# Weight loads of an expert stage with neighbouring rows on one partition, gate and up kept apart

## The chip, the core and the metric

The kernel runs on one core of a Trainium2 chip. The metric is the device time of one execution in microseconds; what is compared is the median of several runs. Engines are PE (TensorE), ACT (ScalarE), DVE (VectorE), POOL (GpSimd) and SP (SyncE, which here only issues transfers). All arithmetic is in float32, the large products in three passes over operands split in a high and a low part.

## What is computed

The reference is one layer of a streaming encoder on 1024 + 64 tokens of width 1024: a layer norm, a token mixing (state space and short convolution), a second layer norm, and a mixture of 64 experts of width 256. Only the experts bear on the change:

```
scores = sigmoid(h @ w_router); top_e, w = 6 of 64 experts for each token, gates normalised * 2.5
for each expert e, over the tokens that chose it:
    hid = silu(x @ w_gate[e]) * (x @ w_up[e])        # 1024 -> 256, twice
    y   = (hid @ w_down[e]) * gate                   # 256 -> 1024
f[token] = sum of its y + shared expert
```

Gate and up weights of an expert are (1024, 256) each, its down weights (256, 1024): 1 MB each, 3 MB for one expert, 192 MB in all.

## The kernel before

The stages follow each other: trunk, mixing, output (which also computes the routing scores, the shared expert and the slot lists), routing, expert, final. The change touches the routing stage and the expert stage.

**Blocks.** Tokens are gathered by expert in blocks of up to 128. An expert has as many blocks as its tokens need, at least one; here 76 blocks, and the loop runs over 77 (an even count of trips after the first). Most experts have one block, some two. Every engine runs the same loop over blocks (`over_blocks`), three of them written out (`HEAD = 3`), the rest in a hardware loop with two blocks a trip.

**Transfers of weights.** SP loads them on its own queue. `raw_up` has three slots (`UP_SLOTS`), each with gate and up of one expert side by side, `raw_dn` two (`DN_SLOTS`). The routing stage issues the loads of experts 0 to 2 (L1514, down of 0 and 1 at L1519), the expert stage the rest (`gate_up` with L1656, `down` with L1664), in the order down of e-3, gate of e, up of e. Before it issues a load, SP waits until the slot is free (`up_l_done`, `dn_l_done`, counted in blocks by a table) and until the load of the same kind for the expert before has landed. A weight matrix is viewed as `(k p) n -> p k n`: row 128k + p goes to partition p. So a partition gets eight rows of 256 values for gate and for up, each row a run of 1 KB, and two rows of 1024 values for down, each a run of 4 KB. In `raw_up` the row k of gate stands next to row k of up, 512 values.

**One block.** ACT copies the weights to `up_h` in two calls of 2048 values a partition (`up_high`, L1687; half 0 has rows k = 0 to 3 of both gate and up, half 1 the others), DVE subtracts to get `up_l` (`up_low`, L1858), both two blocks ahead of the product. `up_high_first` waits for gate and for up before half 0. Down weights are handled alike (`down_high` L1728, `down_low` L1878), in the block itself. PE's order in a block n (`body`) is: `up(n)`, 24 matmuls of 128 x 512 (L1801); `turn_x(n+1)`, 8 transposes of the gathered tokens (L1820), where the token tile `xg` is the operand loaded as weights and the identity is the moving one; `down(n-1)`, 12 matmuls (L1813); `turn_hid(n)`, 2 transposes of the hidden values (L1828). ACT takes the silu of the gate half (L1703) and copies transposes out (L1714, L1720) and results out (L1708); DVE makes `hid` (L1850) and the low parts (L1866, L1872).

**Tokens.** POOL gathers the rows of a block from `tok` by an indirect transfer (L1759) and scatters the results with an addition to `acc` (L1770). These use a queue of their own on the same DMA engines. In POOL's order of a block stand the scatter of block n-1 and then the gather of block n+3; a scatter is issued only when the scatter before has landed, since both may add to the same rows. PE's `turn_x` waits for the gather.

Of the kernel before, what the change touches and what calls it, by code (L numbers as in the profile page):

```python
# [6 lines left out]
ALU = mybir.AluOpType  # L7
ACT = mybir.ActivationFunctionType
F32 = mybir.dt.float32
F32R = mybir.dt.float32r  # L10
# [3 lines left out]
P = 128  # L14
D = 1024
KD = D // P
# [19 lines left out]
D_EXP = 256  # L36
ROUTED_SCALE = 2.5
IN_RING = 3
UP_SLOTS = 3
# [1450 lines left out]
def routing_stage(nc, io, keep, rt):  # L1490

    with ExitStack() as ctx:
        m = Pools(nc, ctx, "route")
# [14 lines left out]
        @block.sync  # L1508
        def _(sp):
            for e in range(UP_SLOTS):  # L1510
                for side, src, sem in ((0, io.w_gate, rt.gate_in), (1, io.w_up, rt.up_in)):
                    if e:
                        sp.wait_ge(sem, 16 * e)
                    sp.dma_start(rt.raw_up[:, e, :, D_EXP * side:D_EXP * (side + 1)],  # L1514
                                 src[0, e].rearrange("(k p) n -> p k n", p=P)).then_inc(sem, 16)
                if e < DN_SLOTS:
                    if e:
                        sp.wait_ge(rt.down_in, 16 * e)
                    sp.dma_start(rt.raw_dn[:, e, :, :], io.w_down[0, e].rearrange("(k p) n -> p k n", p=P)).then_inc(  # L1519
                        rt.down_in, 16)  # L1520

        @block.gpsimd
# [65 lines left out]
def expert_stage(nc, io, keep, rt):  # L1588

    with ExitStack() as ctx:  # L1590
        m = Pools(nc, ctx, "moe")
        raw_up, raw_dn = rt.raw_up, rt.raw_dn
        up_h, up_l = m.sb("up_h", [P, 2, KD, 2 * D_EXP], F32R), m.sb("up_l", [P, 2, KD, 2 * D_EXP], F32R)
        idx_g, idx_s = m.sb("idx_g", [P, 2], I32), m.sb("idx_s", [P, 2], I32)
        xg = m.sb("xg", [P, 2, D])
        x_h, x_l = m.sb("x_h", [P, 2, KD, P], F32R), m.sb("x_l", [P, 2, KD, P], F32R)
        sg = m.sb("sg", [P, 2, D_EXP])
        hid = m.sb("hid", [P, 2, D_EXP])
# [3 lines left out]
        p_gu = m.ps("p_gu", [P, 2, 512])  # L1602
        p_dn = m.ps("p_dn", [P, 2, 512])
        p_tr = m.ps("p_tr", [P, 2, 512])
        p_ht = m.ps("p_ht", [P, 512])
# [7 lines left out]
        gate_in, up_in, down_in = rt.gate_in, rt.up_in, rt.down_in  # L1613
        go, act_go, sp_go, zeroed = (m.sem(n) for n in ("go", "act_go", "sp_go", "zeroed"))
        block = ctx.enter_context(nc.Block())
        w_g = io.w_gate[0].rearrange("e (k p) n -> e p k n", p=P)
        w_u = io.w_up[0].rearrange("e (k p) n -> e p k n", p=P)
        w_d = io.w_down[0].rearrange("e (k p) n -> e p k n", p=P)
        HEAD = 3
        HALF = KD // 2  # L1620

        def wait(eng, sem, value):

# [24 lines left out]
        @block.sync  # L1648
        def _(sp):
            def gate_up(e, slot, until):  # L1650
                wait(sp, up_l_done, until)
                sp.sem_inc(sp_go, 1)
                for half, src, sem in ((0, w_g, gate_in), (1, w_u, up_in)):
                    wait(sp, sem, e * 16)
                    sp.sem_inc(sp_go, 1)
                    sp.dma_start(raw_up[:, slot, :, D_EXP * half:D_EXP * (half + 1)],  # L1656
                                 src[at(e)].rearrange("a p k n -> (a p) k n")).then_inc(sem, 16)

            def down(e, slot, until):
                wait(sp, dn_l_done, until)  # L1660
                sp.sem_inc(sp_go, 1)
                wait(sp, down_in, e * 16)
                sp.sem_inc(sp_go, 1)
                sp.dma_start(raw_dn[:, slot, :, :], w_d[at(e)].rearrange("a p k n -> (a p) k n")).then_inc(down_in, 16)  # L1664

            def ends(e):
                return entry(sp, 3, e, P)

            AHEAD = UP_SLOTS + DN_SLOTS
            LOOP = UP_SLOTS * DN_SLOTS  # L1670
            peeled = N_EXP - (N_EXP - AHEAD) // LOOP * LOOP
            for e in range(UP_SLOTS, peeled):
                if e >= AHEAD:
                    down(e - UP_SLOTS, (e - UP_SLOTS) % DN_SLOTS, ends(e - AHEAD))
                gate_up(e, e % UP_SLOTS, ends(e - UP_SLOTS))
            with sp.Fori(peeled, N_EXP - LOOP + 1, LOOP) as b:
                for u in range(LOOP):
                    down(b + (u - UP_SLOTS), (peeled + u - UP_SLOTS) % DN_SLOTS, ends(b + (u - AHEAD)))
                    gate_up(b + u, (peeled + u) % UP_SLOTS, ends(b + (u - UP_SLOTS)))
            for e in range(N_EXP - UP_SLOTS, N_EXP):  # L1680
                down(e, e % DN_SLOTS, ends(e - DN_SLOTS))

        @block.scalar
        def _(act):
            def up_high(n, par, slot, half):
                ks = slice(HALF * half, HALF * (half + 1))
                act.activation(up_h[:, par, ks, :],  # L1687
                               raw_up[:, bass.ds(slot, 1), ks, :].rearrange("p a k n -> p (a k) n"),
                               ACT.Copy).then_inc(up_h_done, 1)

            def up_high_first(n, par):
# [100 lines left out]
        @block.tensor  # L1792
        def _(pe):
            def up(n, par):
                wait(pe, xl_done, n + 1)
                wait(pe, up_l_done, n + 1)
                wait(pe, hid_done, n - 1)
                terms = [(x[:, par, k, :], w[:, par, k, :]) for k in range(KD)
                         for x, w in ((x_h, up_h), (x_h, up_l), (x_l, up_h))]
                for i, (x, w) in enumerate(terms):  # L1800
                    mm = pe.matmul(p_gu[:, par, :], x, w, start=(i == 0), stop=(i == len(terms) - 1))  # L1801
                mm.then_inc(up_done, 1)

            def down(n, par):
                wait(pe, dn_l_done, n + 1)
                wait(pe, hidl_done, n + 1)
                wait(pe, y_act, n)
                for h in range(2):
                    cols = slice(512 * h, 512 * (h + 1))
                    terms = [(a[:, par, k, :], w[:, par, k, cols]) for k in range(2)  # L1810
                             for a, w in ((hid_h, dn_h), (hid_h, dn_l), (hid_l, dn_h))]
                    for i, (a, w) in enumerate(terms):
                        mm = pe.matmul(p_dn[:, h, :], a, w, start=(i == 0), stop=(i == len(terms) - 1))  # L1813
                mm.then_inc(down_done, 1)

            def turn_x(n, par):
                wait(pe, gathered[par], dma_count(n, par))
                wait(pe, xl_done, n)
                for k in range(KD):
                    tr = pe.transpose(p_tr[:, k // 4, (k % 4) * P:(k % 4 + 1) * P], xg[:, par, k * P:(k + 1) * P],  # L1820
                                      keep.ident[:, :])
                tr.then_inc(x_turned, 1)

            def turn_hid(n, par):
                wait(pe, hid_done, n + 1)
                wait(pe, hidl_done, n)
                for k in range(2):
                    tr = pe.transpose(p_ht[:, k * P:(k + 1) * P], hid[:, par, k * P:(k + 1) * P], keep.ident[:, :])  # L1828
                tr.then_inc(hid_turned, 1)

            def body(n, par):
                first = isinstance(n, int) and n == 0
                if first:
                    turn_x(0, 0)
                up(n, par)
                turn_x(n + 1, 1 - par)
                if not first:
                    down(n - 1, 1 - par)
                turn_hid(n, par)
            last = over_blocks(pe, body)  # L1840
            down(last + 0, 0)

        @block.vector
        def _(v):
            tt, stt = v.tensor_tensor, v.scalar_tensor_tensor
# [7 lines left out]
            def up_low(n, par, halves=(0, 1)):  # L1853
                slot = entry(v, 1, n, UP_SLOTS - 1)
                for half in halves:
                    ks = slice(HALF * half, HALF * (half + 1))
                    wait(v, up_h_done, n * 2 + (half + 1))
                    low = tt(up_l[:, par, ks, :], raw_up[:, bass.ds(slot, 1), ks, :].rearrange("p a k n -> p (a k) n"),  # L1858
                             up_h[:, par, ks, :].bitcast(F32), ALU.subtract)
                if 1 in halves:  # L1860
                    low.then_inc(up_l_done, 1)

# [107 lines left out]
def build(nc, args):  # L1970

    io = Names()
# [24 lines left out]
    with ExitStack() as ctx:  # L1997
        m = Pools(nc, ctx, "keep")
        keep = Names()
# [32 lines left out]
        with ExitStack() as moe:  # L2032
            r = Pools(nc, moe, "rt")
            rt = Names()
            rt.idx = r.sb("idx", [P, P], I32)
            rt.wgt = r.sb("wgt", [P, P])
            rt.tab = r.sb("tab", [1, 5, P + 8], I32)
            rt.raw_up = r.sb("raw_up", [P, UP_SLOTS, KD, 2 * D_EXP])
            rt.raw_dn = r.sb("raw_dn", [P, DN_SLOTS, 2, D])
            rt.gate_in, rt.up_in, rt.down_in = r.sem("gate_in"), r.sem("up_in"), r.sem("down_in")  # L2040
            routing_stage(nc, io, keep, rt)
            expert_stage(nc, io, keep, rt)
# [32 lines left out]
```

## Time and profile before

| | us |
|---|---|
| median of 3 runs | 1703.79 |
| lowest and highest of them | 1691.95, 1705.31 |
| the profiled execution | 1694.93 |
| its span in the trace | 1693.2 |
| PE busy, with weight loads apart | 1348.9 and 1040.7 |
| DVE, ACT, POOL busy | 1108.3, 829.4, 756.3 |
| moved by DMA | 320.96 MB, mean 190 GB/s |

Busy times are sums over the whole span, and stages with different limits are mixed in them. The busy time of PE counts matmuls whose ends are modelled, so neighbours overlap; the number of matmuls in a window says more of its pace. A DMA share above 1 means that packets overlap on the engines.

### The profile page before, as it was taken

Reading aid. Unit: us, or ns where it says so; the run is one execution under the profiler, and the core shown is the slowest. Engines: PE = TensorE matmul, PEld = TensorE weight load, DVE = VectorE, ACT = ScalarE, POOL = GpSimd, SP = SyncE. Lnnn points to the kernel's source line nnn. Section 1 sums busy time; section 2 is a strip of 40 time slices with the busy share of each in tenths; the row PEclk is TensorE's granted clock in tenths of the full one; section 3 lists DMA queues with packets and bytes.
Section 4 is the critical chain, followed back from the end, with each engine's and each line's share of the span. In section 5 each row is a group of like instructions: output and inputs, shape, how many; then the busy total and the mean of one; then the engine's idle time right before and its main releaser. Section 6 shows DMA issues by size and latency. Waiting matters only on the chain. (4 is left out here: it accounts for less than half of the span.)

```text
span 1693.2 us, 22502 instructions
## 1 busy us (share of the span) xinstructions
PE 1348.9 (80%) x6080; PEld 1040.7 (61%) x6080; DVE 1108.3 (65%) x1480; ACT 829.4 (49%) x911; POOL 756.3 (45%) x811
## 2 busy tenths in 40 slices
PE   1397988987869999509899899998989888888930
PEld 1264656655558888407677677776767676667720
DVE  6931435541546777427878788878778867678858
ACT  2311101101633333017777777777767766767842
POOL 2486532501422333423445555555555545445534
PEclk9998999989879999759999999999999999999965
DMA  8223447244521211167988699979989999998743
GB/s 228 87 53 77 35 68 78 33 57 52 168 76 63 75 55 59 50 224 224 317 272 270 208 334 318 334 243 315 309 252 330 302 312 323 327 315 270 208 130 130
DMA packets 233486, 320.96 MB, mean 190 GB/s; under 512 B 30512, under 2 KB 192304, under 8 KB 233440
## 3 DMA queue, kind: packets, MB, share of 16 engines
q1 hardware_dynamic: 199136, 254.35, 49.9%
q0 software_dynamic: 27488, 63.16, 14.3%
q10 hardware_dynamic: 6816, 2.88, 0.8%
q8 instruction: 22, 0.36, 0.1%
q14 instruction: 24, 0.20, 0.1%
HBM read 282.87 MB, written 64.19 MB: 205 GB/s over the span
## 5 line engine op out<-in xcount | busy, mean ns | idle before, releaser
L1858 DVE TENSOR_TENSOR moe_up_l<-rt_raw_up,moe_up_h 128x2048 fp32r<-128x2048 f32 x158 | 361.4, 2289 | 108.8 <-ACT moe_up_h L1687 108.3
L1687 ACT ACTIVATE moe_up_h<-rt_raw_up 128x2048 fp32r x158 | 301.6, 1910 | 114.4 <-issue 74.8
L1801 PE MATMUL moe_p_gu<-moe_up_h,moe_x_h 128*128 128x512 f32 x616 | 251.9, 409 | 16.2 <-DVE moe_x_l L1866 16.2
L1770 POOL DMA_INDIRECT acc<-moe_y,moe_idx_s x77 | 191.5, 2487 | 134.7 <-DMA acc<-moe_y,moe_idx_s 101.9
L1801 PE MATMUL moe_p_gu<-moe_up_h,moe_x_l 128*128 128x512 f32 x616 | 244.2, 396 | 0.0
L1801 PE MATMUL moe_p_gu<-moe_up_l,moe_x_h 128*128 128x512 f32 x616 | 244.1, 396 | 0.0
L680 PE MATMUL mix_proj<-co_hT,co_win 128*128 128x384 f32 (+1 forms) x768 | 238.7, 473 | 6.5 <-PEq L102 6.5
L1878 DVE TENSOR_TENSOR moe_dn_l<-rt_raw_dn,moe_dn_h 128x2048 fp32r<-128x2048 f32 x77 | 176.8, 2296 | 66.6 <-ACT moe_dn_h L1728 64.2
L680 PEld LDWEIGHTS mix_proj<-co_hT,co_win 128*128 128x128 f32 x768 | 146.7, 192 | 94.9 <-issue 9.6
L1765 POOL COPY moe_idx_s<-rt_idx 128x1 int32 (+1 forms) x77 | 79.5, 1032 | 221.9 <-ACT moe_y L1708 221.9
L1728 ACT ACTIVATE moe_dn_h<-rt_raw_dn 128x2048 fp32r x77 | 148.0, 1922 | 25.1 <-DMA rt_raw_dn<-in_w_down_dram 19.2
L1813 PE MATMUL moe_p_dn<-moe_dn_h,moe_hid_h 128*128 128x512 f32 x308 | 135.4, 440 | 25.1 <-DVE moe_dn_l L1878 25.0
L1801 PEld LDWEIGHTS moe_p_gu<-moe_up_h,moe_x_h 128*128 128x128 f32 x616 | 116.3, 189 | 48.6 <-DVE moe_x_l L1866 23.7
L1820 PE MATMUL moe_p_tr<-keep_ident,moe_xg 128*128 128x128 f32 x624 | 86.4, 283 | 69.9 <-DMA moe_xg<-tok,moe_idx_g 69.7
L1759 POOL DMA_INDIRECT moe_xg<-tok,moe_idx_g x80 | 111.3, 1391 | 65.9 <-POOL moe_idx_g L1756 62.0
L1714 ACT ACTIVATE moe_x_h<-moe_p_tr 128x512 fp32r<-128x512 f32 x156 | 84.7, 596 | 101.8 <-PE moe_p_tr L1820 97.4
L1801 PEld LDWEIGHTS moe_p_gu<-moe_up_h,moe_x_l 128*128 128x128 f32 x616 | 116.1, 189 | 28.2
L1801 PEld LDWEIGHTS moe_p_gu<-moe_up_l,moe_x_h 128*128 128x128 f32 x616 | 116.6, 189 | 24.7
L1820 PEld LDWEIGHTS moe_p_tr<-keep_ident,moe_xg 128*128 128x128 f32 x624 | 72.2, 144 | 92.6 <-DMA moe_xg<-tok,moe_idx_g 87.5
L1813 PE MATMUL moe_p_dn<-moe_dn_l,moe_hid_h 128*128 128x512 f32 x308 | 127.7, 415 | 0.0
L1813 PE MATMUL moe_p_dn<-moe_dn_h,moe_hid_l 128*128 128x512 f32 x308 | 127.6, 414 | 0.0
L1866 DVE TENSOR_TENSOR moe_x_l<-moe_p_tr,moe_x_h 128x512 fp32r<-128x512 f32 x156 | 100.2, 684 | 21.1 <-ACT moe_x_h L1714 19.0
(399 smaller groups left out, 2332.2 us busy)
## 6 DMA issues: line engine op xcount, KB each, us to landing
rt_raw_up<-in_w_gate_dram SPq DMA_DIRECT2D x64, 1024.0 KB
rt_raw_up<-in_w_up_dram SPq DMA_DIRECT2D x64, 1024.0 KB
rt_raw_dn<-in_w_down_dram SPq DMA_DIRECT2D x64, 1024.0 KB
co_win<-in_w_in_dram SPq DMA_DIRECT2D x16, 512.0 KB
resid<-trunk_x SPq DMA_DIRECT2D x9, 512.0 KB, 2.6
proj_res<-resid SPq DMA_DIRECT2D x9, 512.0 KB
tok<-proj_x POOLq DMA_DIRECT2D x9, 512.0 KB
acc<-proj_x POOLq DMA_DIRECT2D x9, 512.0 KB
```

Source lines behind the costliest of these rows:

```text
L680: mm = pe.matmul(proj[:, pn % 3, 0:ln], win[:, i % RING, k, :], hT[:, k, lo:lo + ln], start=(k == 0), stop=(k == KD - 1))
L1687: act.activation(up_h[:, par, ks, :], raw_up[:, bass.ds(slot, 1), ks, :].rearrange("p a k n -> p (a k) n"), ACT.Copy).then_inc(up_h_done, 1)
L1714: act.activation(x_h[:, par, 4 * h:4 * h + 4, :], p_tr[:, h, :].rearrange("p (k t) -> p k t", k=4), ACT.Copy).then_inc(xh_done, 1)
L1728: act.activation(dn_h[:, par, :, :], raw_dn[:, bass.ds(slot, 1), :, :].rearrange("p a k n -> p (a k) n"), ACT.Copy).then_inc(dn_h_done, 1)
L1759: pool.indirect_dma_start(out=xg[:, par, :], out_offset=None, in_=io.tok, in_offset=bass.IndirectOffsetOnAxis(ap=idx_g[:, par:par + 1], ax ...
L1770: pool.indirect_dma_start(out=io.acc, in_=y[:, par, :], in_offset=None, out_offset=bass.IndirectOffsetOnAxis(ap=idx_s[:, par:par + 1], axi ...
L1801: mm = pe.matmul(p_gu[:, par, :], x, w, start=(i == 0), stop=(i == len(terms) - 1))
L1813: mm = pe.matmul(p_dn[:, h, :], a, w, start=(i == 0), stop=(i == len(terms) - 1))
L1820: tr = pe.transpose(p_tr[:, k // 4, (k % 4) * P:(k % 4 + 1) * P], xg[:, par, k * P:(k + 1) * P], keep.ident[:, :])
L1858: low = tt(up_l[:, par, ks, :], raw_up[:, bass.ds(slot, 1), ks, :].rearrange("p a k n -> p (a k) n"), up_h[:, par, ks, :].bitcast(F32), AL ...
L1866: low = tt(x_l[:, par, 4 * h:4 * h + 4, :], p_tr[:, h, :].rearrange("p (k t) -> p k t", k=4), x_h[:, par, 4 * h:4 * h + 4, :].bitcast(F32) ...
L1878: tt(dn_l[:, par, :, :], raw_dn[:, bass.ds(slot, 1), :, :].rearrange("p a k n -> p (a k) n"), dn_h[:, par, :, :].bitcast(F32), ALU.subtrac ...
```

## The change

The views of the weights become `(p k) n -> p k n`: partition p gets the rows 8p to 8p + 7 of gate and of up, one run of 8 KB each, and the rows 2p and 2p + 1 of down, also 8 KB. In `raw_up`, `up_h` and `up_l` gate and up stand apart, each with its eight rows in one piece; the two calls of a copy or a subtraction take gate and up in place of the lower and the upper rows. A matmul of the up product reads row k of both, two runs of 256 values. As the inner index of the products is now 8p + k (2p + k for down), the transposes take each eighth column of `xg` from k on and each second of `hid`.

```diff
@@ routing stage
-                    sp.dma_start(rt.raw_up[:, e, :, D_EXP * side:D_EXP * (side + 1)],
-                                 src[0, e].rearrange("(k p) n -> p k n", p=P)).then_inc(sem, 16)
+                    sp.dma_start(rt.raw_up[:, e, side, :, :],
+                                 src[0, e].rearrange("(p k) n -> p k n", p=P)).then_inc(sem, 16)
...
-                    sp.dma_start(rt.raw_dn[:, e, :, :], io.w_down[0, e].rearrange("(k p) n -> p k n", p=P)).then_inc(
+                    sp.dma_start(rt.raw_dn[:, e, :, :], io.w_down[0, e].rearrange("(p k) n -> p k n", p=P)).then_inc(
@@ expert stage
-        up_h, up_l = m.sb("up_h", [P, 2, KD, 2 * D_EXP], F32R), m.sb("up_l", [P, 2, KD, 2 * D_EXP], F32R)
+        up_h, up_l = m.sb("up_h", [P, 2, 2, KD, D_EXP], F32R), m.sb("up_l", [P, 2, 2, KD, D_EXP], F32R)
...
-        w_g = io.w_gate[0].rearrange("e (k p) n -> e p k n", p=P)
-        w_u = io.w_up[0].rearrange("e (k p) n -> e p k n", p=P)
-        w_d = io.w_down[0].rearrange("e (k p) n -> e p k n", p=P)
+        w_g = io.w_gate[0].rearrange("e (p k) n -> e p k n", p=P)
+        w_u = io.w_up[0].rearrange("e (p k) n -> e p k n", p=P)
+        w_d = io.w_down[0].rearrange("e (p k) n -> e p k n", p=P)
...
-                    sp.dma_start(raw_up[:, slot, :, D_EXP * half:D_EXP * (half + 1)],
+                    sp.dma_start(raw_up[:, slot, half, :, :],
...
-                ks = slice(HALF * half, HALF * (half + 1))
-                act.activation(up_h[:, par, ks, :],
-                               raw_up[:, bass.ds(slot, 1), ks, :].rearrange("p a k n -> p (a k) n"),
+                act.activation(up_h[:, par, half, :, :],
+                               raw_up[:, bass.ds(slot, 1), half, :, :].rearrange("p a k n -> p (a k) n"),
...
-                terms = [(x[:, par, k, :], w[:, par, k, :]) for k in range(KD)
+                terms = [(x[:, par, k, :], w[:, par, :, k, :]) for k in range(KD)
...
-                    mm = pe.matmul(p_gu[:, par, :], x, w, start=(i == 0), stop=(i == len(terms) - 1))
+                    mm = pe.matmul(p_gu[:, par, :].rearrange("p (a n) -> p a n", a=2), x, w, start=(i == 0), stop=(i == len(terms) - 1))
...
-                    tr = pe.transpose(p_tr[:, k // 4, (k % 4) * P:(k % 4 + 1) * P], xg[:, par, k * P:(k + 1) * P],
+                    tr = pe.transpose(p_tr[:, k // 4, (k % 4) * P:(k % 4 + 1) * P], xg[:, par, k:D:KD],
...
-                    tr = pe.transpose(p_ht[:, k * P:(k + 1) * P], hid[:, par, k * P:(k + 1) * P], keep.ident[:, :])
+                    tr = pe.transpose(p_ht[:, k * P:(k + 1) * P], hid[:, par, k:D_EXP:2], keep.ident[:, :])
...
-                    ks = slice(HALF * half, HALF * (half + 1))
...
-                    low = tt(up_l[:, par, ks, :], raw_up[:, bass.ds(slot, 1), ks, :].rearrange("p a k n -> p (a k) n"),
-                             up_h[:, par, ks, :].bitcast(F32), ALU.subtract)
+                    low = tt(up_l[:, par, half, :, :],
+                             raw_up[:, bass.ds(slot, 1), half, :, :].rearrange("p a k n -> p (a k) n"),
+                             up_h[:, par, half, :, :].bitcast(F32), ALU.subtract)
...
-            rt.raw_up = r.sb("raw_up", [P, UP_SLOTS, KD, 2 * D_EXP])
+            rt.raw_up = r.sb("raw_up", [P, UP_SLOTS, 2, KD, D_EXP])
```

## Rows read from the trace of the kernel before

**Rows 1.** The page: DMA share in 40 slices of the span, and packets.
```profile
DMA  8223447244521211167988699979989999998743
...
DMA packets 233486, 320.96 MB, mean 190 GB/s; under 512 B 30512, under 2 KB 192304, under 8 KB 233440
```
**Rows 2.** Instructions of line L1703, the silu, one for each block.
```profile
L1703 ACT ACTIVATE moe_sg<-moe_p_gu x77: 357/383/392, 770.7 to 1613.1; 128x256 f32<-128x256 f32 x77
```
**Rows 3.** Windows: us; PE, PEld, DVE, ACT, POOL busy (count); PE clock, DMA share, GB/s.
```profile
1573.52:1613.13 39.61, 38.89 (x186) 30.97 (x185) 35.10 (x29) 32.94 (x33) 22.15 (x17) 1.00 0.56 155
...
1338.08:1508.40 170.32, 148.47 (x648) 117.17 (x647) 122.41 (x100) 115.02 (x113) 84.88 (x58) 0.93 1.01 318
...
770.66:1613.13 842.47, 755.51 (x3486) 600.25 (x3485) 662.01 (x531) 624.01 (x608) 429.46 (x300) 0.98 0.92 288
```
**Rows 4.** Timeline of SP: first and last gate load of the saturated stretch.
```profile
1338.08 0.37 SPq L1656 DMA_DIRECT2D rt_raw_up<-in_w_gate_dram  x1
...
1508.40 0.37 SPq L1656 DMA_DIRECT2D rt_raw_up<-in_w_gate_dram  x1
```
**Rows 5.** Waits from 780 to 1640 us: total us, times, longest.
```profile
POOL acc L1770 <- DMA acc<-moe_y,moe_idx_s: 101.9, 42, 4.7
...
PE moe_p_tr L1820 <- DMA moe_xg<-tok,moe_idx_g: 53.6, 38, 3.1
...
ACT moe_up_h L1687 <- DMA rt_raw_up<-in_w_up_dram: 23.9, 21, 4.0
...
ACT moe_dn_h L1728 <- DMA rt_raw_dn<-in_w_down_dram: 19.2, 17, 3.2
ACT moe_up_h L1687 <- DMA rt_raw_up<-in_w_gate_dram: 15.7, 17, 4.0
```
**Rows 6.** Waits of SP's queue, whole span.
```profile
SPq L1652 <- DVE moe_up_l L1858: 197.6, 34, 19.9
```
**Rows 7.** DMA from 741.6 to 744.4 us, then from 747.8 to 748.9 us.
```profile
DMA packets 966, 0.98 MB, mean 351 GB/s; under 512 B 13, under 2 KB 964, under 8 KB 966
...
q1 hardware_dynamic: 966, 0.98, 109.1%
...
DMA packets 111, 0.44 MB, mean 401 GB/s; under 512 B 1, under 2 KB 4, under 8 KB 111
...
q1 hardware_dynamic: 111, 0.44, 100.6%
```
**Rows 8.** Timeline of SP: loads of the routing stage, start us and us.
```profile
739.53 0.37 SPq L1514 DMA_DIRECT2D rt_raw_up<-in_w_up_dram  x1
742.48 0.37 SPq L1519 DMA_DIRECT2D rt_raw_dn<-in_w_down_dram  x1
745.49 0.37 SPq L1514 DMA_DIRECT2D rt_raw_up<-in_w_gate_dram  x1
748.49 0.37 SPq L1514 DMA_DIRECT2D rt_raw_up<-in_w_up_dram  x1
```
**Rows 9.** Groups by line, whole span: busy us, mean ns; idle before.
```profile
L1858 DVE TENSOR_TENSOR moe_up_l<-rt_raw_up,moe_up_h 128x2048 fp32r<-128x2048 f32 x158 | 361.4, 2289 | 108.8 <-ACT moe_up_h L1687 108.3
...
L1801 PE MATMUL moe_p_gu<-moe_up_h,moe_x_h 128*128 128x512 f32 x616 | 251.9, 409 | 16.2 <-DVE moe_x_l L1866 16.2
...
L1801 PE MATMUL moe_p_gu<-moe_up_h,moe_x_l 128*128 128x512 f32 x616 | 244.2, 396 | 0.0
...
L1820 PEld LDWEIGHTS moe_p_tr<-keep_ident,moe_xg 128*128 128x128 f32 x624 | 72.2, 144 | 92.6 <-DMA moe_xg<-tok,moe_idx_g 87.5
...
L269 PEld LDWEIGHTS trunk_pst<-keep_ident,trunk_x 128*128 128x128 f32 x72 | 14.1, 223 | 33.8 <-POOL trunk_x L239 33.8
```
**Rows 10.** Timeline of POOL, two scatters, and of PE's weight loads, one block's transposes.
```profile
998.28 1.85 POOL L1770 DMA_INDIRECT acc<-moe_y,moe_idx_s  x1 [2.67 <-DMA acc<-moe_y,moe_idx_s]
...
1008.95 2.08 POOL L1770 DMA_INDIRECT acc<-moe_y,moe_idx_s  x1 [2.35 <-DMA acc<-moe_y,moe_idx_s]
...
1010.42 0.86 PEld L1820 LDWEIGHTS moe_p_tr<-keep_ident,moe_xg 128*128 128x128 f32 x8 [1.76 <-DMA moe_xg<-tok,moe_idx_g]
```

More of the change, by code:

```diff
@@ L1615, in expert_stage @@
         block = ctx.enter_context(nc.Block())
-        w_g = io.w_gate[0].rearrange("e (k p) n -> e p k n", p=P)
-        w_u = io.w_up[0].rearrange("e (k p) n -> e p k n", p=P)
-        w_d = io.w_down[0].rearrange("e (k p) n -> e p k n", p=P)
+        w_g = io.w_gate[0].rearrange("e (p k) n -> e p k n", p=P)
+        w_u = io.w_up[0].rearrange("e (p k) n -> e p k n", p=P)
+        w_d = io.w_down[0].rearrange("e (p k) n -> e p k n", p=P)
         HEAD = 3
-        HALF = KD // 2
         def wait(eng, sem, value):
```

## The prediction

> **What bounds the kernel now.** I read the page first for where the DMA engines are busy, then the expert stage in windows, then who waits for whom, then single instructions. The page shows the DMA engines nearly full from the middle of the span to shortly before its end, and 192,304 of 233,486 packets under 2 KB [rows 1]. This is the expert stage: 77 blocks, whose silu steps start from 770.7 to 1613.1 us, so 76 periods in 842.5 us, 11.08 us each [rows 2]. Three windows of it tell three things [rows 3]. From 1573.52 to 1613.13, when the weights are all but loaded (DMA share 0.56), PE holds 186 matmuls; a block has 24 + 12 + 8 + 2 = 46, so this is four blocks in 39.61 us, 9.90 us each, and PE is busy 38.89 us of it: PE in its own order is the floor. From 1338.08 to 1508.40 the DMA share is 1.01 at 318 GB/s and PE has 648 matmuls, 14 blocks in 170.32 us. There each expert has one block, and the first and last gate load of the stretch, 14 experts apart, stand at just these times [rows 4]: 12.17 us for each expert, set by the transfers. What is left, 842.5 - 170.3 = 672.2 us for 62 blocks, runs at 10.84 us, between the two. The waits name what fills it [rows 5]: ACT waits 23.9 + 15.7 + 19.2 us for weights to land, PE 53.6 us for the gathered tokens, and POOL 101.9 us for the scatter before, so the token transfers are late as well when the same engines carry weights. SP on the other hand waits 197.6 us for a free up slot [rows 6]: with experts of two blocks the loads are far enough ahead, and faster ones bring nothing there.
>
> **The transfers.** Edits of the loads (L1514, L1519, L1656, L1664 and the three views) turn 1 KB runs of gate and up into 8 KB, and 4 KB runs of down into 8 KB; bytes, issues and waits stay. Today's price is in two quiet windows [rows 7]. One holds only 1 KB packets: 351 GB/s, so with 16 engines one per 16 x 1.024/351 = 46.7 ns. The other holds nearly only 4 KB packets: 401 GB/s; 111 packets take 100.6% of 16 engines for 1.1 us, 159.5 ns each. An expert costs 2 x 1.049/0.351 = 5.98 us for gate and up and 256 x 159.5/16 = 2.55 us for down, 8.53 us. The trace shows no 8 KB load, so its cost is bounded. From above: 8 KB at the 4 KB rate, 3 x 2.55 = 7.66 us, 0.9 less. From below: the share of the 1 KB window (109.1% of 2.8 us for 966 packets) makes 50.6 ns a packet; the line through this and 159.5 ns has 36.3 ns per KB and gives 305 ns for 8 KB, 384 x 305/16 = 7.32 us, against 2048 x 50.6/16 + 2.55 = 9.03 us, 1.7 less. The line through 46.7 and 159.5 ns gives 310 ns, 7.44 us, 1.09 less. I take **1.1 us for each expert**, since 46.7 ns is the spacing that really passed.
>
> A rule speaks against this. The Trainium skill, DMA: Bandwidth & Descriptors, section Bandwidth, says that for loads from HBM the HBM side binds at about 358 GB/s for a core. By it 351 GB/s would leave 2% and nearly nothing would come of the change. The 4 KB window's 401 GB/s disagrees on this lone core, so I keep this case only as a rival.
>
> What becomes of it: in the saturated stretch every microsecond of transfer is one of time, as 12.17 - 1.1 = 11.07 us still lies over the floor of 9.90: 14 x 1.1 = **15.4 us**. In the other 62 blocks, some 45 experts (64, less 14 and those loaded before 770 us) lose 1.1 us each, 49.5 us of transfer, and the blocks stand 62 x (10.84 - 9.90) = 58 us over the floor. This can't all come back: between experts of two blocks SP waits for slots, and the token transfers keep their latency. Bounds are 0 and 49.5 us; I take a bit under half, **22 us**, as the waits for weights and those for tokens are of like size and only the first shrink by themselves. In the routing stage the first loads follow each other at 2.95 to 3.01 us [rows 8], and the stage ends only when SP has issued the last one at 748.49, since SP is behind all other engines there. Four of the loads before that have 1 KB runs: 4 x (3.0 - 2.6) = **1.5 us**.
>
> **The split of gate and up** (layouts of raw_up, up_h, up_l; L1682 to L1690, L1852 to L1859). Each ACT copy and each DVE subtraction (2289 ns [rows 9]) keeps 2048 contiguous elements. The first copy now needs gate alone, but up_high_first still waits for both, so nothing starts earlier; no wait is added either: 0. The 24 matmuls of L1801 read two runs of 256 in place of one of 512. The trace has no such read. It can't be faster than one run, and the nearest rows for what an operand may cost are the two kinds of this very matmul, 396 and 409 ns [rows 9]: 13 ns x 24 x 77 = 24 us as the upper end, as all of it would be on PE's path. I take 0, because each run is still 1 KB long.
>
> **The transposes.** The contraction is permuted, so L1820 now loads columns of xg 32 bytes apart (8 per block) and L1828 columns of hid 8 bytes apart (2 per block). They are on PE's path, between the up and the down product. Eight loads take 0.86 us together, 108 ns each [rows 10]. No strided load stands in the trace, and a stride can't make one faster. Bounds: 0, and by the slowest rows of the same load of 128 columns, 223 ns in the trunk against 144 here [rows 9], about 1.5 times, 0.5 us a block; as that row is no stride either, the rivals go to twice (+0.86 us a block) and beyond. I take 0: the load has 108 ns for 128 elements, 0.84 ns each, while the moving side takes in 512 elements in at most 396 ns, 0.77 ns each, so the weight side reads with time to spare.
>
> The Trainium skill, Advanced Engine Details and Errata, section Memory Cachelines, has a rule the other way: SBUF lines have 16 bytes, and an access to a new line each time is penalised unless two hits fall in a line. By it the 8-byte steps of hid are free and the 32-byte steps of xg pay. No run here shows it yet; by it the sum would be the first rival.
>
> **Sum.** 15.4 + 22 + 1.5 = 38.9 us. The profiled execution took 1694.93 us (span 1693.2), which gives 1656. It lies 0.5% under the median of the runs, 1703.79; scaled by 1656/1694.93 = 0.977 this is **1665 us**.
>
> **Rivals.** (1) The stride doubles the eight loads: floor 9.90 + 0.86 = 10.76 us. The stretch keeps its gain, but the 62 blocks can't go under 10.76 and have some 0.3 us of leftover waits: 62 x (11.06 - 10.84) = +14, so 14 - 15.4 - 1.5 = -3 us, scaled 1700. For: PE is the floor. Against: element rate above. (2) The slower side: the strided loads cost over twice, at three times +1.7 us a block, floor 11.6, 76 x 11.7 = 889 against 842.5, +47 - 1.5, scaled 1750; with +1.3 it is 1719. It decides from about +1.1 us a block, where the floor of 11.0 meets today's 11.08. (3) Packets of 8 KB delay the token transfers on the same engines: a scatter waits for the landing of the one before. Its starts at 998.28 and 1008.95 are 10.67 us apart with 2.35 us of that wait, and then PE waits 1.76 us for the gather before its transposes [rows 10]. If each scatter and gather pair lost 0.6 us (a packet of 8 KB before it where one of 1 or 4 KB was), the blocks outside the stretch would go from 10.84 to 11.25 us and the stretch keep half its gain: 25 - 8 - 1.5 = +16, scaled 1720. Against: engines free up 1.1 us sooner per expert. (4) 8 KB packets move no faster than 1 KB ones in a mix limited to 318 GB/s by the memory: only the 1.5 us of the routing stage, 1702.
>
> **How the numbers follow.** Forecast 0.60, (1) 0.13, (2) 0.08, (3) 0.09, (4) 0.10. The forecast's own range: without the 22 and at 0.9 us an expert 1694.93 - 14.1, scaled 1690; with all of 49.5 and 1.7 us an expert 1628; I cut it to 1642 as the floor makes the last part unlikely. The whole range takes in (1), (4) and part of (2) and (3): 1642 to 1716. A measurement here tells about 1% from no change. Faster by more: nearly all of the forecast and a little of (1), (4): 0.64. Within 1%: 0.19. Slower: (2), most of (3): 0.17.
>
> **What would show it.** Right: nearly no packets under 2 KB in the expert stage, q1 with 64 x (2048 - 256 + 256 - 128) = 122,880 packets fewer; the stretch at about 11.1 us an expert; waits of ACT for weights well below 58.8 us; eight weight loads of L1820 still in 0.86 us; first gate loads of the routing stage closer together. Wrong: loads of L1820 at twice their time with PE busy through each block (1, 2); PE's wait for the gather and POOL's for the scatter grown (3); packets of 8 KB above 360 ns each (4).

## The result and the profile after

The changed kernel takes 1757.1 us (median of 4 runs, 1753.4 to 1761.55), the kernel before 1700.65 us (median of 4 runs beside them): a ratio of 1.034, with a 95% interval of 1.029 to 1.039. The forecast was 1665 us. The profiled execution took 1753.4 us with a span of 1751.6. The kernel became slower, although its loads, where they run alone, became just as fast as forecast. Both belong together.

The page of the changed kernel: DMA share in 40 slices, packets, the two large queues (packets, MB, share of 16 engines), and groups of section 5.

```profile
DMA  7213437425512111369785887878778889977633
...
DMA packets 110606, 320.96 MB, mean 183 GB/s; under 512 B 30512, under 2 KB 61232, under 8 KB 85984
...
q1 hardware_dynamic: 76256, 254.35, 44.0%
q0 software_dynamic: 27488, 63.16, 14.5%
...
L1799 PE MATMUL moe_p_gu<-moe_up_h,moe_x_h 128*128 128x512 f32 x616 | 250.9, 407 | 10.7 <-DVE moe_x_l L1864 10.7
...
L1799 PE MATMUL moe_p_gu<-moe_up_h,moe_x_l 128*128 128x512 f32 x616 | 243.5, 395 | 0.0
```

There are 233,486 - 110,606 = 122,880 packets fewer [rows 1], the number forecast. But the DMA share is lower in most slices of the expert stage: the engines that were the bound in a part of it now stand idle in part. The matmuls take as long as before [rows 9].

The silu of the changed kernel, one for each block (min/median/max ns, first and last start), against [rows 2].

```profile
L1701 ACT ACTIVATE moe_sg<-moe_p_gu x77: 352/384/387, 765.4 to 1671.2; 128x256 f32<-128x256 f32 x77
```

Windows of the changed kernel, with the columns of [rows 3]: the whole stage, the 14 experts of the forecast's saturated stretch, three blocks near the end.

```profile
765.36:1671.17 905.81, 778.92 (x3486) 627.24 (x3485) 663.69 (x532) 627.39 (x607) 445.10 (x300) 0.95 0.80 268
1372.28:1546.72 174.44, 142.94 (x635) 113.99 (x633) 122.94 (x99) 115.58 (x112) 74.29 (x55) 0.95 0.89 310
1639.65:1671.17 31.52, 29.50 (x138) 23.62 (x137) 26.84 (x23) 24.68 (x25) 19.37 (x13) 1.00 0.48 119
```

The stage grew from 842.5 to 905.8 us, 63.3 us, which is more than all of the span's 58.4. In the stretch an expert takes 174.44/14 = 12.46 us where it took 12.17, and the engines no longer fill it (0.89 for 1.01). Something else sets the pace there, and the waits name it. Waits of the changed kernel from 780 to 1700 us (total us, times, longest), as in [rows 5].

```profile
PE moe_p_tr L1818 <- DMA moe_xg<-tok,moe_idx_g: 117.2, 53, 5.2
...
POOL acc L1768 <- DMA acc<-moe_y,moe_idx_s: 72.3, 30, 4.8
...
ACT moe_up_h L1685 <- DMA rt_raw_up<-in_w_up_dram: 0.9, 2, 0.5
ACT moe_up_h L1685 <- DMA rt_raw_up<-in_w_gate_dram: 0.5, 1, 0.5
ACT moe_dn_h L1726 <- DMA rt_raw_dn<-in_w_down_dram: 0.3, 1, 0.3
```

ACT's waits for weights fell from 58.8 to 1.7 us. PE's wait for gathered tokens grew from 53.6 to 117.2 us. With the windows this makes a balance of the stage. PE was idle for 842.5 - 755.5 = 87.0 us, of which 53.6 for tokens and 33.4 for all else; it is idle for 905.8 - 778.9 = 126.9 us now, 117.2 for tokens and 9.7 for all else. So the rest gave 23.7 us back and the tokens took 63.6. The third part is in PE's busy time, 23.4 us more for as many matmuls. 63.6 - 23.7 + 23.4 = 63.3 us.

One stall of the changed kernel, one of its longest: POOL's, SP's and PE's instructions from its timeline.

```profile
1405.49 3.51 POOL L1768 DMA_INDIRECT acc<-moe_y,moe_idx_s  x1 [0.93 <-POOL moe_idx_s L1763]
...
1407.89 0.33 SPq L1663 DMA_DIRECT2D rt_raw_dn<-in_w_down_dram  x1
...
1410.09 0.33 SPq L1655 DMA_DIRECT2D rt_raw_up<-in_w_gate_dram  x1
...
1410.57 1.06 POOL L1757 DMA_INDIRECT moe_xg<-tok,moe_idx_g  x1 [0.80 <-POOL moe_idx_g L1754]
...
1410.79 0.33 SPq L1655 DMA_DIRECT2D rt_raw_up<-in_w_up_dram  x1
...
1420.36 1.90 POOL L1768 DMA_INDIRECT acc<-moe_y,moe_idx_s  x1 [4.83 <-DMA acc<-moe_y,moe_idx_s]
...
1423.34 1.57 PEld L1818 LDWEIGHTS moe_p_tr<-keep_ident,moe_xg 128*128 128x128 f32 x8 [5.59 <-DMA moe_xg<-tok,moe_idx_g]
```

Three weight loads, down, gate and up, are issued within 3 us of the gather. PE's transposes of that gather's tokens start 1423.34 - 1410.57 = 12.8 us after its issue, 5.59 of them waited. In the block of [rows 10], before the change, it is 1010.42 - 1001.68 = 8.7 us, the latter being this row of that kernel's timeline:

```profile
1001.68 1.05 POOL L1759 DMA_INDIRECT moe_xg<-tok,moe_idx_g  x1 [0.79 <-POOL moe_idx_g L1756]
```

This pair is not the mean: over the stage the median from a gather's issue to its landing is 10.4 us in the changed kernel and, by the landings in the trace, 8.1 us before. The scatter here too waits for the landing of the one before, 14.87 us after it where it was 10.67 [rows 10], and the next gather is issued only behind it. In sum, however, POOL's wait for the scatter before fell, from 101.9 to 72.3 us; it is the gather that became later. The eight loads after the stall take 1.57 us, which leads to the clock. Two windows of the changed kernel, with the stall and behind it (the number before the DMA share is the granted clock):

```profile
1404.00:1424.00 20.00, 13.34 (x62) 10.46 (x61) 14.54 (x12) 11.55 (x11) 9.88 (x8) 0.98 0.93 338
1424.00:1434.00 10.00, 10.00 (x44) 8.30 (x43) 5.23 (x5) 7.67 (x7) 2.87 (x4) 0.86 0.82 287
```

Behind this stall part of the time runs at 1.2 GHz in place of 2.4. The clock records show the same at 16 of the 17 places in the stage where PE waited over 3 us. The time at the lower level is 96 us of the stage where it was 41 us before, and the mean granted clock 0.95 where it was 0.98. At half speed the 55 us more cost up to 27 us, an estimate of enough size for the 23.4 us that PE is busy longer.

### The profile page after: what moved, and what is told of

Same layout as the page of the kernel before. It is cut to its first block and busy times, and to the rows that moved or that the text cites. A ratio compares the mean times of both kernels' runs of the same rounds, so it can differ in the third digit from the quotient of the medians.

```text
span 1751.6 us, 22502 instructions
## 1 busy us (share of the span) xinstructions
PE 1369.3 (78%) x6080; PEld 1065.9 (61%) x6080; DVE 1110.4 (63%) x1480; ACT 832.5 (48%) x911; POOL 771.6 (44%) x811
## 2 busy tenths in 40 slices
DMA packets 110606, 320.96 MB, mean 183 GB/s; under 512 B 30512, under 2 KB 61232, under 8 KB 85984
## 5 line engine op out<-in xcount | busy, mean ns | idle before, releaser
L1768 POOL DMA_INDIRECT acc<-moe_y,moe_idx_s x77 | 210.6, 2735 | 116.1 <-DMA acc<-moe_y,moe_idx_s 72.3
L1818 PE MATMUL moe_p_tr<-keep_ident,moe_xg 128*128 128x128 f32 x624 | 101.6, 314 | 129.6 <-DMA moe_xg<-tok,moe_idx_g 129.6
L1763 POOL COPY moe_idx_s<-rt_idx 128x1 int32 (+1 forms) x77 | 71.5, 929 | 288.7 <-ACT moe_y L1706 288.7
L1818 PEld LDWEIGHTS moe_p_tr<-keep_ident,moe_xg 128*128 128x128 f32 x624 | 86.8, 198 | 155.2 <-DMA moe_xg<-tok,moe_idx_g 153.1
L1811 PE MATMUL moe_p_dn<-moe_dn_h,moe_hid_h 128*128 128x512 f32 x308 | 141.8, 460 | 6.9 <-DVE moe_dn_l L1876 6.9
L1799 PEld LDWEIGHTS moe_p_gu<-moe_up_h,moe_x_l 128*128 128x128 f32 x616 | 115.7, 188 | 28.5
L1811 PE MATMUL moe_p_dn<-moe_dn_l,moe_hid_h 128*128 128x512 f32 x308 | 132.1, 429 | 0.0
L1811 PE MATMUL moe_p_dn<-moe_dn_h,moe_hid_l 128*128 128x512 f32 x308 | 131.6, 427 | 0.0
```

Source lines behind the costliest of these rows:

```text
L1768: pool.indirect_dma_start(out=io.acc, in_=y[:, par, :], in_offset=None, out_offset=bass.IndirectOffsetOnAxis(ap=idx_s[:, par:par + 1], axi ...
L1799: mm = pe.matmul(p_gu[:, par, :].rearrange("p (a n) -> p a n", a=2), x, w, start=(i == 0), stop=(i == len(terms) - 1))
```

## The experiments

My theory (Q in the expectations): packets of 8 KB on the weight queue take time on the same 16 engines from the token queue, and POOL's order (gather behind a waiting scatter) turns that delay into idle time of PE. The rival theories: the strided transposes cost the time (S); the order in which the rows are read from memory does; or it is the loads' earlier issue, at whatever packet length. PE's wait for the gather stands in the table at the end of this section.

**The stride alone, and 8 KB without it.** In the first the before kernel gets the strided transposes; in the second the changed kernel loses them. In both the products take rows in another order than the weights lie, so the numbers computed differ, not the amount of work.

```diff
@@ stride_only, on the kernel before; no_stride is the reverse edit on the kernel after
-                    tr = pe.transpose(..., xg[:, par, k * P:(k + 1) * P], ...)
+                    tr = pe.transpose(..., xg[:, par, k:D:KD], ...)
-                    tr = pe.transpose(..., hid[:, par, k * P:(k + 1) * P], ...)
+                    tr = pe.transpose(..., hid[:, par, k:D_EXP:2], ...)
```

> Kernel before with its loads as they were, but the transposes read each eighth column of xg and each second of hid (so the products take rows in the wrong order). Theory Q (packets of 8 KB hold up the token transfers, the stride is small): eight loads at 0.97 us instead of 0.86 and two at 0.43 instead of 0.37, 0.17 us a block, at most 13 us: ratio to before 1.000 to 1.008. Theory S (the strided loads are what costs): ratio 1.02 to 1.034.

> Changed kernel with contiguous transposes (products take rows in the wrong order). Theory Q: ratio to before 1.025 to 1.034, PE's wait for the gather stays above 100 us. Theory S: ratio at most 1.005 and the wait goes.

Measured: stride alone 1699.37 us, where the kernel before took 1695.43 us beside it, ratio 1.002 (1.000 to 1.004). Groups of stride_only (busy us, mean ns), against 144 ns in [rows 9]:

```profile
L1820 PEld LDWEIGHTS moe_p_tr<-keep_ident,moe_xg 128*128 128x128 f32 x624 | 79.8, 192 | 83.1 <-DMA moe_xg<-tok,moe_idx_g 79.5
...
L1828 PEld LDWEIGHTS moe_p_ht<-keep_ident,moe_hid 128*128 128x128 f32 x154 | 30.2, 197 | 6.7 <-DVE moe_hid L1850 0.3 <-issue 0.2
```

The mean record is a third longer, 192 ns for 144, but the records overlap: eight in a row take 0.97 us where they took 0.86.

8 KB without the stride: 1752.70 us, ratio 1.036 (1.031 to 1.040), as slow as the whole change and just above the 1.034 that theory Q allowed. Its wait, from 780 to 1640 us:

```profile
PE moe_p_tr L1818 <- DMA moe_xg<-tok,moe_idx_g: 119.3, 49, 6.1
```

The loads are dearer by the stride, but the stride is not the cause: rivals (1) and (2) fall.

**The packet length.** Everything of the change stays but the length of a run. A gap in `raw_up` and `raw_dn` breaks it into pieces, of 4 KB (gap 64 bytes), or of 2 KB for gate and up and 4 KB for down (gap 32 bytes). runs_1k keeps the layout of before for gate and up (1 KB) with the new views and transposes, and 8 KB for down.

```diff
@@ runs_4k; runs_2k has [P, UP_SLOTS, 2, 4, D_HALF + 8], [P, DN_SLOTS, 2, D + 8] and q=4 for gate and up
-            rt.raw_up = r.sb("raw_up", [P, UP_SLOTS, 2, KD, D_EXP])
+            rt.raw_up = r.sb("raw_up", [P, UP_SLOTS, 2, 2, D + 16])
-            rt.raw_dn = r.sb("raw_dn", [P, DN_SLOTS, 2, D])
+            rt.raw_dn = r.sb("raw_dn", [P, DN_SLOTS, 2, D + 16])
...
-        w_g = io.w_gate[0].rearrange("e (p k) n -> e p k n", p=P)
+        w_g = io.w_gate[0].rearrange("e (p q k) n -> e p q (k n)", p=P, q=2)
...
-                    sp.dma_start(raw_up[:, slot, half, :, :],
+                    sp.dma_start(raw_up[:, slot, half, :, 0:D],
```

> Changed kernel, but each 8 KB of a partition stands in two pieces of 4 KB with a gap of 64 bytes, so that packets have 4 KB; all else as in the changed kernel. Theory Q: the token queue gets its share back, PE's wait for the gather falls to 50 to 80 us, ratio to before 0.98 to 1.01. Theory S, or that the order of rows in memory costs: ratio stays at 1.034.

> Kernel before with neighbouring rows on one partition but gate and up side by side, so that packets of gate and up have 1 KB again (down 8 KB); strided transposes. Theory Q: about as stride_only, 1.000 to 1.012. Theory S: 1.02 to 1.034. If the order of rows in memory costs, it shows here as more than stride_only.

> Changed kernel with gate and up in four pieces of 2 KB a partition and down in two of 4 KB, gaps of 32 bytes between. Theory Q (how much the token queue gets depends on the length of the weight packets): gathers move at a rate between that of 4 KB packets (16.6 packets of 4 KB in half a microsecond) and that of 1 KB (20.6), PE's wait for the gather 55 to 80 us, ratio to before 0.998 to 1.006. Rival (only 8 KB packets are special): gathers as with 4 KB, ratio 1.006.

Measured: 4 KB 1706.36 us, ratio 1.006 (1.0035 to 1.009); 1 KB 1702.95 us, 1.006 (1.003 to 1.008); 2 KB 1677.96 us, 0.986 (0.981 to 0.990), the three with PE waits of 80.4, 58.6 and 55.5 us for the gather. From 2 KB on the wait grows with the length, and the time with the wait. The wait alone does not give the time: runs_1k and runs_4k are equally slow at 58.6 and 80.4 us. 2 KB lies below the range of both theories (0.998 to 1.006, and 1.006), so its gain was forecast by neither; it is faster than the kernel before. It has most of the cheaper transfer, as the window below shows, and leaves the gather's wait where it was; ACT's waits for weights are 38.0 us for 58.8. DMA of runs_2k from 736 to 738 us, weights of 2 KB packets alone:

```profile
DMA packets 407, 0.82 MB, mean 409 GB/s; under 512 B 8, under 2 KB 8, under 8 KB 407
```

runs_1k differs from the kernel before by the order of rows in memory, the stride and the 8 KB packets of down. Together these cost 0.6%: it waits more for the gather (58.6 us for 53.6) and for the scatter (138.5 for 101.9) and a little less for weights (53.8 for 58.8). So the order of rows, which every one of these kernels has, is not the cause of the 3.4% either.

How the engines divide themselves is to be seen in windows of 1.5 us in which a gather runs beside weight loads (q1: weights, q0: tokens; packets, MB, share of 16 engines). The kernel before, 942.5 to 944:

```profile
DMA packets 325, 0.58 MB, mean 387 GB/s; under 512 B 28, under 2 KB 235, under 8 KB 325
...
q1 hardware_dynamic: 254, 0.35, 65.5%
q0 software_dynamic: 71, 0.23, 39.2%
```

runs_2k, 975.25 to 976.75, and then runs_4k, 996.25 to 997.75:

```profile
q1 hardware_dynamic: 194, 0.40, 67.9%
q0 software_dynamic: 123, 0.22, 37.7%
```

```profile
q1 hardware_dynamic: 102, 0.41, 67.7%
q0 software_dynamic: 52, 0.20, 32.3%
```

The changed kernel, 920.75 to 922.25:

```profile
DMA packets 107, 0.63 MB, mean 418 GB/s; under 512 B 10, under 2 KB 10, under 8 KB 51
...
q1 hardware_dynamic: 59, 0.46, 72.2%
q0 software_dynamic: 48, 0.17, 27.4%
```

In sum more bytes pass, 418 GB/s for 387, but the tokens' share of the engines falls from 39.2 to 27.4%. The packet records of the whole stage say the same. Token records of 4 KB are of two kinds, with medians of 159 ns for the gathers and some 328 ns for the scatters with their addition. In slices of half a microsecond with weight packets, no scatter record and at least eight gather records, the gather records are 20.4 a slice in the kernel before, 19.3 with 2 KB, 16.7 with 4 KB and 13.5 with 8 KB. (Slices with five or more give lower numbers in the same order: 18.8, 17.9, 15.7, 12.3.) A single gather record still takes 159 ns in all four kernels, which speaks against a memory that answers more slowly: fewer of them get their turn. The median from a gather's issue to its landing is 8.1, 8.0, 8.6 and 10.4 us in this order.

The Trainium skill, DMA: Bandwidth & Descriptors, section Queues, rings and completion order, says that each engine goes round the queues that have work, a whole packet of one before the next. The direction of the four windows agrees. How long a turn is remains open: a packet there holds several descriptors, and the records do not show where one ends. Turns of single records it is not, as the tokens' share of the bytes beside 1, 2, 4 and 8 KB would then be 4/5, 2/3, 1/2 and 1/3, and the windows have 0.40, 0.35, 0.33 and 0.27.

**POOL's order.** If the delay hurts because the gather stands behind a waiting scatter, putting it ahead should bring the lost gain to light.

```diff
-                if not first:
-                    scatter(n - 1, 1 - par)
                 gather(n + 3, 1 - par)
+                if not first:
+                    scatter(n - 1, 1 - par)
```

> Changed kernel, but POOL issues the gather of block n+3 before the scatter of block n-1 instead of behind it. Theory Q (with 8 KB packets the gather lands too late, being issued behind a scatter that waits for the one before): PE's wait for the gather falls from 117 us to under 20, ratio to before 0.96 to 0.985. Rival (something else of the 8 KB loads holds the blocks up, as the scatter chain alone): the wait goes elsewhere and the ratio stays above 1.02.

> Kernel before with the same swap. Theory Q: its 54 us of waits for the gather go, but the loads of 1 KB packets (ACT's 59 us of waits for weights) bind: ratio 0.97 to 0.99, above the one of the changed kernel with the swap. Rival: ratio 0.995 to 1.005, the order of the two does nothing here.

> The kernel with 4 KB packets and the swap. Theory Q: its 80 us of waits for the gather go, ratio 0.96 to 0.98, as good as the changed kernel with the swap or 0.5% better, since scatters are served sooner. Rival: as with 8 KB packets without the swap, above 1.0.

> The same with the gather ahead of the scatter. Theory Q: between 4 KB and 1 KB packets with the swap (0.969 and 0.989), nearer to the first, 0.970 to 0.978. Rival (shorter packets are better whenever the loads keep up): below 0.969.

Measured: with 8 KB 1654.84 us, 0.975 (0.971 to 0.980); the kernel before with this edit alone 1675.37 us, 0.989 (0.986 to 0.992); with 4 KB 1643.55 us, 0.969 (0.966 to 0.973); with 2 KB 1643.57 us, 0.968 (0.963 to 0.973). The last lies below the 0.970 to 0.978 of theory Q and in the range of its rival, that shorter packets are better whenever the loads keep up; its interval takes in both, and 2 and 4 KB can't be told apart here. Waits of the 8 KB one, from 780 to 1640 us:

```profile
POOL acc L1768 <- DMA acc<-moe_y,moe_idx_s: 242.5, 60, 7.2
...
ACT moe_y L1706 <- DMA acc<-moe_y,moe_idx_s: 44.0, 31, 2.9
...
PE moe_p_tr L1818 <- DMA moe_xg<-tok,moe_idx_g: 11.5, 13, 1.9
```

PE's wait for the gather went from 117.2 to 11.5 us, and the time by 102 us, from 1757.1 to 1654.84. The delay did not vanish: it moved to the scatter, for which POOL waits 242.5 us and now even ACT, before it writes results into the buffer that the scatter still reads. Most of this is beside PE's work: over the stage PE is idle for 804.8 - 748.8 = 56.0 us, where it was 126.9. The same waits of the kernel before with this edit:

```profile
ACT moe_up_h L1687 <- DMA rt_raw_up<-in_w_up_dram: 49.9, 24, 4.7
ACT moe_dn_h L1728 <- DMA rt_raw_dn<-in_w_down_dram: 35.3, 21, 4.2
...
ACT moe_up_h L1687 <- DMA rt_raw_up<-in_w_gate_dram: 14.8, 16, 4.5
```

Its gather makes PE wait no more, and the weights are the next in line, 100 us of waits. Here longer runs help: 1654.84 against 1675.37 us on the same chip, 1.2% less, with 8 KB. So the change's sign hangs on the order of two lines in POOL's program.

| packets of gate and up (down: 4 KB, in the last row 8 KB) | order of before: ratio | PE waits for gather, us | gather first: ratio |
|---|---|---|---|
| 1 KB (kernel before) | 1 | 53.6 | 0.989 |
| 2 KB | 0.986 | 55.5 | 0.968 |
| 4 KB | 1.006 | 80.4 | 0.969 |
| 8 KB (the change) | 1.034 | 117.2 | 0.975 |

2 or 4 KB with the gather first are the fastest kernels of the study, about 3% under the kernel before. Windows of the 2 KB one over its expert stage:

```profile
767.96:1560.80 792.84, 746.69 (x3488) 608.84 (x3487) 658.35 (x531) 622.03 (x608) 442.52 (x302) 0.99 0.92 306
```

792.8 us for 76 periods are 10.43 us a block, PE is busy for 746.7 of them, and the clock stays at 0.99.

## Why the prediction was wrong

**The price of a transfer: right.** The forecast had 310 ns for a packet of 8 KB and 1.09 us less for an expert. DMA of the changed kernel from 734.5 to 737 us, with no token transfers:

```profile
DMA packets 149, 1.07 MB, mean 429 GB/s; under 512 B 18, under 2 KB 18, under 8 KB 18
...
q1 hardware_dynamic: 149, 1.07, 101.6%
```

131 of the packets are of 8 KB: 16 engines x 2.5 us x 1.016/131 = 310 ns at most, as the 18 short ones are counted in. The page rule that HBM binds at about 358 GB/s (Trainium skill, DMA: Bandwidth & Descriptors, Bandwidth) disagrees with the 429 GB/s of this lone core, and the measurement decides; the 425 GB/s that the same section gives for a single core's 16 MB transfers agrees. Rival (4) falls.

**The saturated stretch, -15.4 us: its gain came, and a term of +25 us was missing.** With the same 14 experts in both windows, it came out 4.1 us longer (174.44 against 170.32). PE's wait for tokens in the two windows, before and after:

```profile
PE moe_p_tr L1820 <- DMA moe_xg<-tok,moe_idx_g: 3.4, 2, 2.0
...
PE moe_p_tr L1818 <- DMA moe_xg<-tok,moe_idx_g: 28.5, 13, 5.2
```

All the rest of PE's idle time there fell from 170.32 - 148.47 - 3.4 = 18.5 to 174.44 - 142.94 - 28.5 = 3.0 us. That is 15.5 us less, just what the term had. Its busy time fell by 5.5 us more. But the wait for tokens, which the sum had at nothing in this stretch, grew by 25.1 us: 25.1 - 15.5 - 5.5 = 4.1. The step took the DMA share of 1.01 for proof that only bytes count there. A share over all queues does not say which transfer is late.

**The other 62 blocks, -22 us: the step that failed most.** It said that "the waits for weights and those for tokens are of like size and only the first shrink by themselves". The first do shrink, but they were waits of ACT (58.8 us, 34.5 of them inside the stretch), and PE's idle time held less than 22 us of them. Outside the stretch PE waited 50.2 us for tokens before and was idle for 14.9 us otherwise; that rest became 6.7 us, a gain of 8.2. So most of the 58 us over the floor was the wait for tokens. The step held that wait constant, and it grew by 38.5 us there, to 88.7, and by 63.6 us in the whole stage. PE's busy time, which the sum left as it was, grew by 28.9 us outside the stretch.

**Rival (3), given 0.09 and 1720 us, is what happened, and its price was too low.** I had charged 0.6 us for a scatter and gather pair, the length of one packet more ahead of it, and let 0.41 us of it reach a block without a working for that. The gather doesn't wait for one packet once: it shares the engines with the longer ones for as long as it runs, and its rate falls by a third (20.4 to 13.5 records in half a microsecond). In the median this is 2.3 us more from the gather's issue to its landing, and in the two timelines above 4.1 us to the transposes. One of the two signs named for this rival came, PE's wait for the gather; the other, a grown wait of POOL for the scatter, did not (101.9 to 72.3 us). "Engines free up 1.1 us sooner per expert", which I set against the rival, did not help the tokens. Two amplifiers were not in the sum. In POOL's order the gather stands behind the scatter, whose results come from PE, so a delay can come round again; how much comes round is not measured, but that the swap takes back 102 us shows that this order was needed for the loss. And PE ran longer at the lower clock: without the stride, no_stride still has 773.6 us of PE busy in the stage against 755.5, 18.1 us more at a granted clock of 0.94.

**The routing stage, -1.5 us: right.** From the first load to the last SP took 748.49 - 730.66 = 17.8 us before and 744.71 - 728.04 = 16.7 us after, 1.2 us less. Two loads of the changed kernel's stage:

```profile
735.26 0.33 SPq L1514 DMA_DIRECT2D rt_raw_up<-in_w_up_dram  x1
...
737.76 0.33 SPq L1519 DMA_DIRECT2D rt_raw_dn<-in_w_down_dram  x1
```

They stand 2.5 us apart where it was 3.0 [rows 8]; one gap of 4.49 us elsewhere takes part of the gain.

**The split of gate and up, 0: right.** Two runs of 256 cost nothing: 407 and 395 ns against 409 and 396 [rows 9].

**The strided transposes, 0: a small miss.** The eight loads take 0.97 us, against 0.86 [rows 10], and the two of the hidden values 0.43 against 0.37, late in the stage, where the granted clock is 1.00:

```profile
1629.61 0.97 PEld L1818 LDWEIGHTS moe_p_tr<-keep_ident,moe_xg 128*128 128x128 f32 x8 [3.34 <-DMA moe_xg<-tok,moe_idx_g]
...
1633.13 0.43 PEld L1826 LDWEIGHTS moe_p_ht<-keep_ident,moe_hid 128*128 128x128 f32 x2
```

That is 0.17 us a block, 13 us if all of it were on the path; stride_only shows 1699.4 against 1695.4 us, 4 us, so most of it is taken out of waits. The rule of the Trainium skill (Advanced Engine Details and Errata, Memory Cachelines) is half right here: the 32-byte steps pay 0.11 in 0.86 us, but the 8-byte steps, free by the rule, pay 0.06 in 0.37.

**Open.** Not tried apart is the moment of the weight loads. SP waits less for landings than before and more for free slots, as here in the changed kernel, so its loads come in bursts just when a slot is freed.

```profile
SPq L1660 <- DVE moe_dn_l L1876: 403.1, 50, 12.2
SPq L1651 <- DVE moe_up_l L1855: 270.4, 57, 22.5
```

With 4 KB these waits are 293.6 and 253.8 us and the loss is a sixth; with 2 KB they are 161.4 and 230.7 us, still above the 100.7 and 197.6 of the kernel before, and there is no loss. Nor did the gathers come to lie beside weights only by the change: 96.5% of their records fall in half microseconds with weight packets before, 94.6% after. Both speak for the length of a packet as the larger part, but do not give the bursts a number. How an engine chooses between its queues is open as well.

## What to carry to other kernels

Here longer packets made their queue faster and, from 4 KB on, its neighbour on the same engines slower. So before lengthening the bulk transfers, look for small transfers with a deadline beside them, and give these slack first, by issuing the one that the bottleneck engine waits for ahead of anything that itself waits. A DMA share near 1 says that engines are full, not whose packets are late; the waits of the bottleneck engine say that. And the longest packet was not the best: in the order of before it was 2 KB, with the gather first 2 or 4 KB.

## What the runs showed of the hardware

- Packets of 8 KB took 310 ns, 429 GB/s in a window with loads alone; 1 KB gave 351 and 4 KB 401 GB/s [rows 7], and 2 KB 409 GB/s in runs_2k. Most of the gain in rate is had at 2 KB.
- Beside other traffic, the rate of gathered 4 KB token packets fell from 20.4 to 13.5 in half a microsecond as the packets of the other queue grew from 1 to 8 KB; at 2 KB it was still 19.3. Each of them took 159 ns throughout; those of a scatter with addition took some 328 ns.
- A run of TensorE weight loads with strided columns took 13% longer at 32-byte steps (0.97 for 0.86 us) and 16% at 8-byte steps (0.43 for 0.37 us).
- A wait of PE of 5.15 us was followed by a granted clock of 0.86 over the next 10 us. In the changed kernel's expert stage the clock fell to the lower level at 16 of the 17 waits of PE over 3 us, so such a wait cost more than its own length.
